# A feed-forward layer whose up product is made by Strassen's seven half-size products, with its activations passed through DRAM

## The reference

```python
D_MODEL = 1024; BATCH = 1; SEQ = 2048; D_FF = 4 * D_MODEL        # all float32
def reference(x, mem, ...):
    # input projection, a diagonal state-space scan, stick-breaking attention
    # (8 heads of 64), output projection, cross-attention over 256 tokens
    ...
    h = rmsnorm(x, g_mlp[l])
    x = x + jnp.square(jax.nn.relu(h @ w_up[l])) @ w_down[l]
    return x
```

## Time and profile before

| | |
|---|---|
| median of 3 runs | 3311.54 us (3311.31 to 3315.63) |
| the profiled execution | 3312.09 us, span 3310.3 us |
| `mlp` in the span | from 1849 us to the end, 1461 us |
| its PE, first transpose / first up matmul / last matmul | 1859.05 / 1874.23 / 3305.3 us |
| PE busy over the whole span | 91% |
| DVE, ACT, GpSimd (POOL) busy | 52%, 33%, 15% |
| mean granted PE clock | 0.955 |
| attention: first DMA issued, first matmul | 642.80, 660.45 us |

### The profile page before, as it was taken

One profiled execution on the slowest core, in us unless ns is written; L12 is line 12 of the kernel. 1 busy time (PEld: TensorE's weight loads), 2 busy tenths in 40 slices (PEclk: granted clock), 3 DMA queues, 4 the chain that ended last, 5 costly groups with the idle time before them and its releaser, 6 DMA issues. The chain is left out here.

```text
span 3310.3 us, 42553 instructions
## 1 busy us (share of the span) xinstructions
PE 3008.5 (91%) x15810; PEld 2545.5 (77%) x15810; DVE 1717.8 (52%) x2404; ACT 1106.8 (33%) x1839; POOL 494.4 (15%) x397
## 2 busy tenths in 40 slices
PE   6999936599999969986999699999999999999998
PEld 5888824488988957764888588888887788888887
DVE  5333257587877855436565444444444544444444
ACT  4333215376766752213343221111111211111111
POOL 1212113455555532110000000000000000000000
PEclk9999967899999989997999899999999999999999
DMA  4232252362242033324222521111111411111111
GB/s 163 83 92 73 77 79 43 86 167 55 49 101 54 11 80 102 95 93 155 71 85 69 202 65 51 50 38 51 42 47 52 165 51 38 51 51 51 51 38 64
DMA packets 230220, 251.36 MB, mean 76 GB/s; under 512 B 107457, under 2 KB 181185, under 8 KB 230081
## 3 DMA queue, kind: packets, MB, share of 16 engines
q1 hardware_dynamic: 230096, 249.74, 25.8%
HBM read 189.79 MB, written 58.73 MB: 75 GB/s over the span
## 5 line engine op out<-in xcount | busy, mean ns | idle before, releaser
L2595 DVE TENSOR_TENSOR f_y<-f_ps_down,f_y 128x1024 f32<-128x1024 f32 x256 | 313.2, 1224 | 324.9 <-PE f_ps_down L2705 324.8
L2538 ACT ACTIVATE f_act_f<-f_ps_up 128x512 f32<-128x512 f32 x128 | 76.5, 598 | 1032.0 <-PE f_ps_up L2689 1032.0
L2687 PE MATMUL f_ps_up<-f_ht_hi,f_up_hi 128*128 128x512 f32 x1024 | 401.2, 392 | 6.4 <-DVE f_act_f L2612 6.4
L2703 PE MATMUL f_ps_down<-f_down_hi,f_a_hi 128*128 128x512 f32 x1024 | 400.4, 391 | 6.1 <-issue 6.1
L2688 PE MATMUL f_ps_up<-f_ht_lo,f_up_hi 128*128 128x512 f32 x1024 | 400.4, 391 | 0.0
L2689 PE MATMUL f_ps_up<-f_ht_hi,f_up_lo 128*128 128x512 f32 x1024 | 400.3, 391 | 0.0
L2705 PE MATMUL f_ps_down<-f_down_hi,f_a_lo 128*128 128x512 f32 x1024 | 400.0, 391 | 0.0
L2704 PE MATMUL f_ps_down<-f_down_lo,f_a_hi 128*128 128x512 f32 x1024 | 400.0, 391 | 0.0
L690 POOL TENSOR_TENSOR a_w<-a_on,a_left 128x640 f32<-128x640 f32 (+5 forms) x192 | 282.1, 1469 | 254.6 <-DVE a_left L740 114.6
L2612 DVE SCALAR_TENSOR_TENSOR f_act_f<-f_ps_up,f_act_f 128x512 f32<-128x512 f32 x128 | 88.5, 691 | 395.3 <-ACT f_act_f L2538 395.3
L828 PE MATMUL a_ps_y<-a_wt,a_v 128*96 128x128 f32 x2176 | 270.6, 274 | 5.2 <-DVE a_yt L763 5.2
(11 more groups left out here) (352 smaller groups left out, 5505.9 us busy)
## 6 DMA issues: line engine op xcount, KB each, us to landing
f_up_raw<-in_w_up SPq DMA_DIRECT2D x32, 1024.0 KB, 5.3
f_down_raw<-in_w_down SPq DMA_DIRECT2D x32, 1024.0 KB, 4.8
p_xt<-in_x SPq DMA_DIRECT2D x16, 512.0 KB, 4.8
q<-p_qt SPq DMA_DIRECT2D x16, 512.0 KB, 3.2
k<-p_qt SPq DMA_DIRECT2D x16, 512.0 KB, 3.2
a_q<-q SPq DMA_DIRECT2D x16, 512.0 KB, 5.6
a_k_hi<-k SPq DMA_DIRECT2D x32, 256.0 KB, 8.4
a_k_lo<-k SPq DMA_DIRECT2D x32, 256.0 KB, 9.3
```

Of the source, the lines that this page charges most:

```text
L2595: dve.tensor_tensor(y[:, t, :], down_ps[t % 2][:, :], y[:, t, :], ALU.add).then_inc(added.sem, 1)
L2687: pe.matmul(o, up_hi[:, k, cols], ht_hi[:, k, rows], start=(k == 0), stop=False)
L2703: pe.matmul(o, a_hi[par][:, s, rows], down_hi[:, s, cols], start=(s == 0), stop=False)
```

## The change

**The up product.** A block is still 256 columns of `w_up` by 1024 rows, but it is cut in two along the depth, the columns and the rows. Of the four quarters of the weight block DVE makes four sums (`S1` to `S4`, L2769 to L2782), and of the four quarters of h, once a chunk, four sums in place (`T1` to `T4`). Seven products of half depth (four slices by three matmuls, 12 matmuls of 512 columns, L2935 to L2937) are made per block, in the order ONE, TWO, SIX, SEVEN, FOUR, FIVE, THREE, each in one of four PSUM banks. The high and low parts of all seven variants of h are kept in `big`; those of the seven variants of the weight are made anew for each block, one slot of `big` each. DVE combines the products with seven additions (`R11`, `u2`, `R22`, `R21`, `R22`, `u2`, `R12`) into four tiles in `xr`; ACT takes relu and square (`activate`), and SP stores each tile, 256 KB, to the DRAM scratch `a`.

**The down product** comes after all 32 up blocks, as 256 steps in straight-line code: two halves of the output columns, in each four groups of 512 rows, in each 32 depth slices. A step is 12 matmuls of 512 columns. `a` is read back (512 KB for two steps) and split by ACT and DVE into a ring of three slots; the half of `w_down` is loaded and split during the half's first group (512 KB for two steps) and stays in `big`. Each group sums its whole depth in four PSUM banks, and DVE adds x once per group and tile.

**Around them.** ACT scales the rows now, and g_mlp is multiplied in when DVE copies a transposed tile out of PSUM (`copy_h`). The second chunk's rows are normed, transposed and copied in blocks 1 to 8; their T sums are made by GpSimd; their seven variants are split in blocks 15 and 16.

**Attention.** The first 512 columns of `q` and `k` of the first pair are loaded first, under a semaphore of their own, then the half's `v`, then columns 512 to 1023.

```diff
+            def load_begin(cols, done_q, done_k):
+                for a in range(2):
+                    sp.dma_start(q2[a][:, cols].bitcast(F32), q_dram[a, :, cols]).then_inc(done_q, DMA)
+                    for dst, part in ((k2_hi[a][0], 0), (k2_lo[a][0], 1)):
+                        for copy in range(2):
+                            sp.dma_start(dst[copy * HEAD:(copy + 1) * HEAD, cols].bitcast(F32),
+                                         k_dram[a, part * HEAD:(part + 1) * HEAD, cols]).then_inc(done_k, DMA)
+            load_begin(slice(0, BANK), begin_loaded, begin_loaded)
...
+            load_begin(slice(BANK, HALF), q_loaded[0], k_loaded[0])
...
-                if i in (0, BLOCKS // 2) and first:
+                if s == 0 and i == 0:
+                    pe.wait_ge(begin_loaded, 10 * DMA)
```

SP's program of the up blocks:

```diff
+            def body(b, chunk):
+                if b < LAST:
+                    sp.wait_ge(w_low.sem, w_low.at(b, FOUR + 1))
+                    load_up((b + 1) % BLOCKS)
...
+                store_a(b, chunk, SQ11, 0, 0, 0)
...
+                store_a(b, chunk, SQ21, 3, 1, 0)
+                store_a(b, chunk, SQ22, 2, 1, 1)
+                store_a(b, chunk, SQ12, 1, 0, 1)
```

ACT's program of a block (without what a chunk's change adds), and DVE's:

```diff
+                act.wait_ge(made.sem, made.at(b, ONE + 1))
+                act.wait_ge(combined.sem, combined.at(b - 1, C12))
+                act.activation(u2[:, :], PS_A, ACT.Copy).then_inc(one_copied.sem, 1)
+                    high_w(b + 1, ONE)
+                    high_w(b + 1, TWO)
+                activate(b, R11, C11, SQ11)
+                    high_w(b + 1, SIX)
+                    high_w(b + 1, SEVEN)
+                    norm_x(TILES - 1 + b)
+                    high_w(b + 1, FOUR)
+                activate(b, R21, C21, SQ21)
+                    high_w(b + 1, FIVE)
+                activate(b, R22, C22, SQ22)
+                    high_w(b + 1, THREE)
+                activate(b, R12, C12, SQ12)
```

```diff
+                    low_w(b + 1, ONE)
+                dve.tensor_tensor(R11, PS_B, u2[:, :], ALU.add).then_inc(combined.sem, 1)
+                    sum_one(b + 1)
+                    low_w(b + 1, TWO)
+                dve.tensor_tensor(u2[:, :], PS_C, u2[:, :], ALU.add).then_inc(combined.sem, 1)
+                    sum_two(b + 1)
+                    low_w(b + 1, SIX)
+                dve.tensor_tensor(R22, PS_D, u2[:, :], ALU.add).then_inc(combined.sem, 1)
+                    sum_three(b + 1)
+                    low_w(b + 1, SEVEN)
+                dve.tensor_tensor(R21, PS_A, R22, ALU.add).then_inc(combined.sem, 1)
+                    sum_four(b + 1)
+                    low_w(b + 1, FOUR)
+                dve.tensor_tensor(R22, PS_B, R22, ALU.add).then_inc(combined.sem, 1)
+                dve.tensor_tensor(u2[:, :], PS_B, u2[:, :], ALU.add).then_inc(combined.sem, 1)
+                    low_w(b + 1, FIVE)
+                    copy_h(TILES - 1 + b)
+                dve.tensor_tensor(R12, PS_C, u2[:, :], ALU.add).then_inc(combined.sem, 1)
+                    low_w(b + 1, THREE)
```

More of the change, by code:

```diff
@@ L2354, in mlp @@
     FB = 256
-    S = FB // P
     BLOCKS = D_FF // FB
[L2357 to L2360, removed]
+    ALL = CHUNKS2 * BLOCKS
+    LAST = ALL - 1
+    KH = KC // 2
+    ONE, TWO, SIX, SEVEN, FOUR, FIVE, THREE = range(7)
+    PRODUCTS = 7
+    HV_ORDER = (ONE, TWO, SIX, SEVEN, THREE, FOUR, FIVE)
+    FF_TILES = D_FF // P
+    GROUPS = SEQ // BANK
+    RING = 3
     with ExitStack() as ctx:
@@ L2405, in mlp @@
[L2405 to L2415, removed]
@@ L2417, in turned_into @@
-        def turned_into(n):
-            return down_ps[0][:, :].rearrange("p (k q) -> p k q", q=P) if n < TILES and n % 2 else th_ps[:, :, :]
-        block = ctx.enter_context(nc.Block())
[L2423 to L2437, removed]
+        h_copied = sem("h_copied")
@@ new lines, in is_turning, with boundary_variant @@
+        def is_turning(b, plain):
+            return not plain and TURN_FROM <= b <= TURN_TO
+        BOUNDARY = {(BLOCKS - 1, 1): ONE, (BLOCKS - 1, 3): TWO, (BLOCKS - 1, 4): SIX, (BLOCKS - 1, 5): SEVEN,
+                    (BLOCKS - 1, 6): THREE, (BLOCKS, 0): FOUR, (BLOCKS, 2): FIVE}
+        def boundary_variant(b, slot, plain):
+            return None if plain else BOUNDARY.get((b, slot))
+        STEPS = [(half, g, k) for half in range(2) for g in range(GROUPS) for k in range(FF_TILES)]
@@ L2452, in load_down @@
[L2452 to L2465, removed]
+                if n >= TILES:
+                    sp.wait_ge(h_turned, n - 1)
+                elif n >= 4:
+                    sp.wait_ge(h_turned, n - 3)
@@ L2498, in _ @@
+            store_y(2 * GROUPS - 1)
+            for group in (2 * GROUPS - 2, 2 * GROUPS - 1):
+                for t in range(4):
+                    sp.wait_ge(y_stored[group % 2 * 4 + t], GROUPS * DMA)
         @block.gpsimd
@@ new lines, in add_group @@
+            def add_group(group):
+                dve.wait_ge(y_loaded[group % 2], (group // 2 + 1) * 4 * DMA)
+                for t in range(4):
+                    dve.wait_ge(step_made, (group + 1) * FF_TILES)
+                    dve.tensor_tensor(y_tile(group, t), acc(group, t), y_tile(group, t), ALU.add).then_inc(added, 1)
+            for n, (half, g, k) in enumerate(STEPS):
+                if k == RING and n > RING:
+                    add_group(half * GROUPS + g - 1)
+                low_a(n)
+                if g == 0:
+                    low_down(half, k)
@@ L2725, in _, with product @@
-            program(pe, prologue, up, down, boundary)
+            for n in range(TILES - 2):
+                turn_h(n)
+            def product(b, i, plain):
+                pe.wait_ge(w_low.sem, w_low.at(b, i + 1))
+                if not plain and b % BLOCKS == 0:
+                    pe.wait_ge(hv_low, b // BLOCKS * PRODUCTS + HV_ORDER.index(i) + 1)
+                o = OUT_BANK[i]
+                for k in range(KH):
+                    pe.matmul(o, wv(i, 0)[:, k, :], hv(i, 0)[:, k, :], start=(k == 0), stop=False)
+                    pe.matmul(o, wv(i, 0)[:, k, :], hv(i, 1)[:, k, :], start=False, stop=False)
+                    mm = pe.matmul(o, wv(i, 1)[:, k, :], hv(i, 0)[:, k, :], start=False, stop=(k == KH - 1))
+                mm.then_inc(made.sem, 1)
```

649 lines of the change are left out of this document (414 added, 235 removed).

## The result

The changed kernel takes 3348.48 us in the median of 4 runs (3346.5 to 3349.11), the kernel before 3311.43 (3307.62 to 3315.63). The ratio is 1.0108 with a 95% interval of 1.0092 to 1.0124: slower by about 37 us, where the prediction had 35 us of gain and a range that ended at 3314. The profiled span is 3347.2 us against a forecast of 3274.4, so 72.8 us have to be found.

What follows compares the result with a forecast made beforehand. PE bounds the kernel before; in the new up blocks a 20.0 us load loop over PE's 18.98 decides. Start, up blocks, 694 us of down steps and tail end at 3281.4, less 7 for attention 3274.4; median 3276, range 3236 to 3314.

Steps and rivals of the forecast that it cites:

- In blocks 1 to 8 DVE also copies a transposed tile ...: 21.1 us. PE's own work there is 20.0.: Up blocks 1 to 8: DVE's extra copy, 1.14 us in line, makes the period 21.1 us; eight sum to 168.8.
- gaps of PE long enough to bring the clock down in every block: Up blocks: one of the listed signs that would show the forecast wrong, given no size.
- I take 5.8: Up blocks: landing of the 1 MB weight load, 5.3 us in a quiet queue plus about 0.5, giving 20.0 us a block.
- The walk itself: Up block: from the load's landing through ACT and DVE to the last square, 13.8 us, then 0.4 to issue.
- Loop longer, slower than before: Up blocks: stores delay the load's landing; no gain from 7.1 us on, at 7.5 a time of 3325 us; chance 0.15.
- The change of chunks: Blocks 15 and 16: 30.2 and 26.8 us plus some 10 us lost beside GpSimd, together 67 against 38 of PE work.
- DVE loses about half of the overlap: Blocks 15 and 16: DVE slowed beside GpSimd's three sums of 4.8 us each, some 10 us, bounds 0 and 20.
- The down half: Down product after the up blocks: 256 steps of 2.71 us, 694 us, with 4.2 us ahead of the steps.
- no step was bound by loads: Rival for a half's first group: at 164 GB/s 32 pairs of down steps lose 1.0 us each, 3308 us; chance 0.10.
- Attention: its first matmul: Start of attention: half the columns loaded first, 7 us taken off, bounds 2 and 9; first matmul near 654.
- Block 2's load: Start of the up blocks: its issue at 1919.7, from a landing at 1932.5 less 5.8 and attention's 7.
- The first rival: Up blocks: the load loop hides behind PE, which bounds at 18.98 us a block; 45 us less, 3231 us; chance 0.20.

Runs made afterwards that it cites:

- Experiment 2: Changed kernel with ACT's norm of the x tile moved from behind SEVEN's high part to right behind the copy of ONE: 3307.8 us, 0.9986 of the kernel before.
- experiment 1: Changed kernel with SP issuing the weight load right behind the block's second store instead of its fourth: 3256.02 us, 0.9828 of the kernel before.
- experiment 4: Kernel before with only the new loads at the start of attention: 3306.69 us, ratio 0.9983, 5.2 us less.
- experiment 6: Changed kernel with the load issued ahead of the block's last two stores, still after the last square: 3331.04 us, 1.0053 of the kernel before.
- experiment 7: Changed kernel with early load, norm behind the copy of ONE and T sums on DVE: 3237.92 us, 0.9775 of the kernel before.

## Why the prediction was wrong, by its steps

**The step that failed: "In blocks 1 to 8 DVE also copies a transposed tile ...: 21.1 us. PE's own work there is 20.0."** It walked the loop through SP, the landing, ACT and DVE and added the copy's 1.14 us. It left PE and its order out of the loop: in those blocks PE has an instruction that waits for ACT's norm, ahead of a product that DVE needs, and the norm stands behind a high part that hangs on the load. Measured 27.4, +50.4 us. Experiment 2 takes away this one dependence and gets 40.7 us back; its turning periods of 22.0 to 22.8 are the forecast 21.1 plus the longer landing and some of DVE's line. The prediction's list of what would make it wrong had "gaps of PE long enough to bring the clock down in every block", without a price.

**The mis-sized term: "I take 5.8" for the landing.** The walk itself was right: landing to next issue was 14.2 us on paper and 14.26 in the trace (2401.27 to 2415.53). The landing is 6.48 there. It was worked out from a larger load (0.5 for 256 KB more) and counted one store only. A plain block is 0.9 us over the forecast: 0.7 from the landing, the rest spread over the chain. By the Trainium skill (DMA: Bandwidth & Descriptors, Anatomy of one DMA, the two cost components) 1 MB comes to an estimate of 4.4 us; the page fits these figures on DMAs that GpSimd issues, while SP issues this one, which the prediction did not say. The trace has 2.1 more here, and by that rule PE would have been the bound, which only experiment 1 made true, by another way.

**The rival "Loop longer, slower than before"** named the right loop and sign, and a landing of 7.1 us as its point of decision. It had the wrong cause: at 6.5 the landing alone costs 29 x 0.7 = 20 us and would still have left a gain of some 15. The loss needed the turning blocks.

**What held.** PE at 0.226 us a matmul wherever it is fed. The change of chunks: 68.5 against 67, but not by "DVE loses about half of the overlap": it is held for all of each of three operations, some 4.05 us each, 12.1 in all. The down half came as forecast, 4.04 us of wait ahead of it and some 700 us to the end; no step was bound by loads. Attention: its first matmul came 6.2 us earlier in the changed kernel, and experiment 4 priced it at 5.2 us of the 7.

**What held by luck.** Block 2's load was issued at 1919.17 against 1919.7, by two errors that cancel. In this trace the stage began at 1845.12 against 1848.76 before, 3.6 us earlier and not 7, and from there to that issue it took 74.1 us, 3.9 less than the forecast had (1926.7 less 1848.76 on the old trace's clock).

**The first rival.** It (loop hidden, PE bounds, 3231) is nearly what the kernel does once the load leaves the loop and the norm its place: 3237.92 measured.

## What to carry to other kernels

When a block's period is walked as a loop of waits, walk every engine's own order through it, and ask of every instruction that is in only some of the blocks: what stands in front of it, what stands behind it, and which of these hangs on the loop. A load that has one buffer belongs at the first point at which that buffer is free, not behind the stores of the block. Here that moved it two stores forward and, what counts, off the wait for the last square: 92 us, more than the one product in eight that the change saved (86.7). Moving it as far in the order of DMAs but leaving that wait in front of it (experiment 6, the same order as experiment 1) gave 17. A saving on the bounding engine pays only so long as it stays the bounding one; here PE needed 18.98 us a block and the loop through the other engines 20.9 to 27.4.

## What the runs showed of the hardware

- **DVE beside GpSimd.** A DVE operation that reads two SBUF tiles and starts after a GpSimd one is held until that has ended: 4.68 to 4.76 us for 0.68, all four 0.55 or 0.56 behind its end. GpSimd's own took 4.57 to 4.62, also where a DVE operation with a PSUM input, begun up to 0.23 us ahead of it, still ran beside it (that one took 0.68 as ever; no DVE operation with a PSUM input began inside GpSimd's). The hold goes both ways. In the kernel before, GpSimd's operation that began behind DVE's took 2.26, where the two ahead of it took 1.27 each:

```profile
1202.73 1.22 DVE L1721 TENSOR_TENSOR m_glu_lo<-n_w_raw,m_glu_hi 128x1024 fp32r<-128x1024 f32 x1 [3.75 <-ACT m_glu_hi L1650]
1202.82 2.26 POOL L1601 TENSOR_TENSOR m_g_lo<-m_g,m_g_hi 128x512 fp32r<-128x512 f32 x1
```

That one ended at 1205.08, and DVE's of the earlier trace rows, 1203.88 to 1206.17, ended 1.09 behind it, about its own length and not at half its speed. The Trainium skill (SBUF — State Buffer, who interferes with whom) says of this pair that the second to start is blocked in full; the trace agrees, and the forecast's halving was the wrong model with nearly the right sum.
- **The landing of 1 MB depends on the stores around it, behind it as well as ahead:** 5.3 us in the kernel before, 5.7 with no store behind and one issued 1.8 us ahead, 6.1 with the same and one behind, 6.6 with the last one directly ahead or with two behind it, and 7.0 in experiment 1, with one directly ahead and two more issued 2.4 and 5.1 us behind it (256 KB each).
- **The clock.** After a wait of 4.79 us PE came back at 1.2 GHz: eight transposes in 1.97 us. After a wait of 0.43 they took 1.09, and after none 1.04, at 2.4 GHz. Between these the length of the wait does not decide alone: behind 3.72 they took 1.97 and behind 3.64 1.09 in the same execution, and behind 3.95, in the next block, 1.09 again, with matmuls at 0.63 only from the third on. Over the turning blocks the granted clock was 0.86, and 1.00 in experiment 7.
